# A hybrid decoder layer on one core: the w_out product in seven block products for eight, its transposes and its residual input moved

## The reference

```python
h = rms_norm(x, attn_norm_g)
proj = h @ w_in
...
merged = (jax.nn.sigmoid(g_sb) * (o_sb @ w_branch[:SB_W])
          + jax.nn.sigmoid(g_ds) * (o_ds @ w_branch[SB_W:]))
x = x + merged @ w_out
h = rms_norm(x, ffn_norm_g)
u = causal_depthwise_conv(h @ w_up, conv_w, conv_b)
gate, val = jnp.split(u, 2, axis=-1)
x = x + (jax.nn.silu(gate) * val) @ w_down
```

## Time and profile before

| what | us |
|---|---|
| median of three runs | 1444.48 (1444.48 to 1444.49) |
| the profiled execution | 1446.01 |
| its span | 1444.3 |
| PE busy | 1435.0 (99%) |
| DVE busy | 1097.9 (76%) |
| ACT busy | 827.1 (57%) |
| POOL busy | 437.5 (30%) |

### The profile page before, as it was taken

How to read it: one execution, slowest core, us unless ns; L and a number is a source line. 1 busy time by engine, 2 the same in 40 slices (tenths; PEclk the granted TensorE clock), 3 DMA queues, 4 the chain that set the end, 5 groups by cost and what they waited for, 6 DMA issues and landing times.

```text
span 1444.3 us, 23747 instructions
## 1 busy us (share of the span) xinstructions
PE 1435.0 (99%) x7588; PEld 1228.1 (85%) x7588; DVE 1097.9 (76%) x1468; ACT 827.1 (57%) x1155; POOL 437.5 (30%) x486
## 2 busy tenths in 40 slices
PE   8999999999999999999999999999999999999999
PEld 7888888888888888888888888888888888788887
DVE  6778998886656656765567787777787778899988
ACT  6545677566767766655454554544554545465553
POOL 2310000323232213540015555655556555200000
PEclk9999999999999999999999999999999999999999
DMA  7665665665554555575566666666666665576664
GB/s 246 190 190 162 204 203 179 190 183 176 159 170 149 172 164 183 192 249 184 183 187 177 191 190 190 179 194 189 196 183 187 189 190 188 175 247 205 197 211 146
DMA packets 124358, 272.23 MB, mean 188 GB/s; under 512 B 10784, under 2 KB 10816, under 8 KB 124048
## 3 DMA queue, kind: packets, MB, share of 16 engines
q1 hardware_dynamic: 123520, 269.12, 60.9%
q0 software_dynamic: 464, 2.42, 0.5%
q10 hardware_dynamic: 320, 0.01, 0.0%
HBM read 269.42 MB, written 2.10 MB: 188 GB/s over the span
## 4 chain that ended last, share of the span: by engine, by line
PE 91%; DVE 5%; issue 2%; DMA 1%; POOL 1%; ACT 1%; ACTq 0%; DVEq 0%; SPq 0%; POOLq 0%
PE bank L1950 90%; DVE lo L1149 1%; DVE lo L1549 1%; PE bank L1999 1%; DVE lo L1040 1%; DMA rows_in<-in_attn_norm_g 0%; DMA raw<-in_w_in 0%; POOL u L1914 0%; DMA raw<-in_w_down 0%; ACT hi L583 0%; PE bank L2239 0%; DVE conv L1501 0%; POOL conv L1917 0%; ACT hi L670 0%; DVE y L1639 0%
## 5 line engine op out<-in xcount | busy, mean ns | idle before, releaser
L1040 DVE TENSOR_TENSOR lo<-raw,hi 128x1024 fp32r<-128x1024 f32 (+1 forms) x375 | 484.7, 1298 | 224.1 <-ACT hi L583 223.3
L583 ACT ACTIVATE hi<-raw 128x1024 fp32r<-128x1024 f32 (+1 forms) x375 | 394.0, 1053 | 321.8 <-PE bank L1950 314.7
L1950 PE MATMUL bank<-h2T,hi 128*128 128x512 f32 x1408 | 483.3, 394 | 0.0
L1950 PE MATMUL bank<-h2T,lo 128*128 128x256 f32 x1408 | 376.6, 278 | 0.0
L1950 PEld LDWEIGHTS bank<-h2T,hi 128*128 128x128 f32 x1408 | 257.9, 188 | 53.6
L1950 PE MATMUL bank<-hT,hi 128*128 128x512 f32 (+1 forms) x784 | 273.5, 395 | 0.6 <-DVE qkT L1333 0.6
L1950 PEld LDWEIGHTS bank<-h2T,lo 128*128 128x128 f32 x1408 | 264.4, 188 | 7.8
L1950 PE MATMUL bank<-hT,lo 128*128 128x256 f32 (+1 forms) x784 | 212.9, 281 | 0.0
L1914 POOL TENSOR_TENSOR u<-u,rms_row 128x256 f32<-128x256 f32 x88 | 121.0, 1375 | 239.4 <-DVE u L1491 220.4
L1950 PE MATMUL bank<-hi,ffT 128*128 128x512 f32 x576 | 177.7, 390 | 0.6 <-DVE lo L1549 0.6
L1950 PEld LDWEIGHTS bank<-hT,hi 128*128 128x128 f32 (+1 forms) x784 | 144.0, 187 | 30.5 <-DVE qkT L1333 0.8
(11 more groups left out here) (265 smaller groups left out, 1888.7 us busy)
## 6 DMA issues: line engine op xcount, KB each, us to landing
raw<-in_w_up SPq DMA_DIRECT2D x176, 512.0 KB, 3.8
raw<-in_w_in SPq DMA_DIRECT2D x160, 512.0 KB, 3.6
raw<-in_w_down SPq DMA_DIRECT2D x88, 512.0 KB, 4.4
raw<-in_w_branch SPq DMA_DIRECT2D x32, 512.0 KB, 3.6
raw<-in_w_out SPq DMA_DIRECT2D x32, 512.0 KB, 4.0
raw4h<-in_w_in SPq DMA_DIRECT2D x8, 512.0 KB, 3.6
raw5h<-in_w_in SPq DMA_DIRECT2D x8, 512.0 KB, 4.1
y<-in_x SPq DMA_DIRECT2D x4, 512.0 KB, 6.9
```

The lines of the kernel that those rows point to most:

```text
L583: act.activation(hi[s][:, 0:width], raw[s][:, 0:width], ACT.Copy)\
L1040: dve.tensor_tensor(lo[s][:, 0:width], raw[s][:, 0:width], hi[s][:, 0:width].bitcast(f32), ALU.subtract)\
L1950: return pe.matmul(o, l, r, start=start, stop=stop, skip_group_check=True)
```

## The change

w_out becomes two more blocks, numbered `NB` and `NB + 1`, of eight steps each: four summed pairs (k pairs 0 to 3) alternating with four plain ones (4 to 7). It gets two more `raw` buffers (`raw4m`, `raw5m`), whose first loads wait for the last sigmoids; its sums of `mT` (`left_m`) are made in the branch stage (groups 2 and 3), whose loops are unrolled for that on ACT and DVE. Of x only columns 1024 to 2047 are loaded into `y` at the old place. The first half's banks are copied to `y` by ACT, the far ones added by DVE, and then x's first 1024 columns are added by two accumulating loads from POOL (`x_added`). Of the 16 transposed tiles of `y`, tiles 0 to 3 are made before the last chunk of w_out, the other 12 in pairs behind the first six chunks of the up projection, and the squares for the norm move with them. The first two joins of w_in's last block move from the heads stage to its start. The core of the diff:

```diff
+                        was = (ROW_STEPS + OUT_STEPS)[old // 2]
...
+                        wait_alone(sp, lo_done, (ROWS_AT[2], C_OUT)[stage(step)] - SLOTS + slot + 1)
+                    elif stage(step):
+                        wait_alone(sp, sig_done, 8 * 4)
...
-                    load(slot, raw_rows[slot][:, :],
-                         w_in[kt * P:(kt + 1) * P, ds((2 + NB - 1 - step.m) * BLOCK, BLOCK)])
+                    load(slot, raw_s[stage(step)][slot][:, :],
+                         w[kt * P:(kt + 1) * P, ds(col, BLOCK)])
...
-            with sp.Fori(0, 4) as g:
-                load_group(C_OUT, w_out, CPG * g, GRP * g)
+            for step in OUT_STEPS:
+                load_step(step, w_out, (step.m - NB) * BLOCK)
...
+                if b == NB:
+                    act.activation(y[:, t, h * GRP:(h + 1) * GRP], NEAR[b][o][:, :], ACT.Copy)\
+                        .then_inc(y_out, 1)
+                    return
...
+                    if n >= 2 and j == 3:
+                        left_hi_part(n)
...
+            def square(n, ready, value):
+
+                m, h, t = n // 4, n // 2 % 2, n % 2
+                act.wait_ge(ready, value)
+                act.wait_ge(ss_done, 2 * TH + n - 1)
+                act.activation(junk2[:, t, :], y[:, t, ds(GRP * (2 * m + h), GRP)], ACT.Square,
+                               accum_out=ss[:, t, 2 * m + h:2 * m + h + 1]).then_inc(ss_done, 1)
+
+            for c in range(C_OUT + AHEAD, C_UP + AHEAD):
+                i = c - AHEAD - C_OUT
+                if c == C_UP + 2:
+                    transposed_hi(h2T, KT, 1, [0, 1])
+                chunk_hi(c)
+                if 1 <= i < 5:
+                    merged_hi(3, i - 1)
+                block_out(c)
+                if c == OUT_AT[1] + AHEAD:
+
+                    act.activation(warm[:, :], warm[:, :], ACT.Sqrt).then_inc(passed, 1)
+                if c in (OUT_AT[1] + 19, OUT_AT[1] + 20):
+                    square(c - OUT_AT[1] - 19, x_added[0], 16)
+                if c == C_UP + 2:
+                    transposed_hi(h2T, KT, 1, [2, 3])
...
+                    if not before and 1 <= j < 7:
+                        transposed_hi(h2T, KT, 1, [2 * j + 2, 2 * j + 3])
                     split(C_UP + AHEAD + j, n, 2 * CPG // SLOTS)
                     if before:
                         up_step(n, j)
-                    elif j == 1:
+                    elif j == 0:
+                        square(2, x_added[1], 16)
+                        square(3, x_added[1], 16)
...
+                    if b == NB - 1 and at_ == 2:
+                        join(b, 0)
+                        join(b, 1)
...
-                    if j in (0, 2):
+                    if i and j in (0, 2):
                         join(NB - 1, 2 * i + j // 2)
...
+                    if n >= 2 and j in (0, 1, 2, 4):
+                        {0: sums_whole, 1: sums_diff, 2: sums_rest, 4: sums_lo}[j](n)
+                    weight_sums(c)
...
+            def out_add(m, o, term):
+
+                t, h = o // 2, o % 2
+                cols = y[:, t, (2 * m + h) * GRP:(2 * m + h + 1) * GRP]
+                dve.tensor_tensor(cols, cols, term, ALU.add).then_inc(row_joined, 1)
+
+            def out_sums(m, n):
+
+                one_, five, two, three = far_out[NB + m]
+                if n == 0:
+                    dve.wait_ge(far_copied, 4 * (3 + m) + 4)
+                    dve.tensor_tensor(two[:, :], two[:, :], one_[:, :], ALU.add)\
+                        .then_inc(row_joined, 1)
+                    dve.wait_ge(row_joined, ROW_JOINS + 8 * m + 1)
+                    dve.tensor_tensor(three[:, :], three[:, :], two[:, :], ALU.add)\
+                        .then_inc(row_joined, 1)
...
+            for c in range(C_OUT + AHEAD, C_UP + AHEAD):
+                i = c - AHEAD - C_OUT
+                if c == C_UP + 2:
+                    transposed_lo(h2T, KT, 1, [0, 1])
+                    dve.wait_ge(x_again, 16)
+                    for o in range(4):
+                        wait_full(dve, down_full, 4, 4, o, C_UP)
+                        out_add(1, o, NEAR[NB + 1][o][:, :])
+                    transposed_lo(h2T, KT, 1, [2, 3])
+                chunk_lo(c)
...
+                weight_sums(c)
+                at_ = c - OUT_AT[1]
+                if 0 < at_ < 24 and at_ % 6 == 2:
+                    out_sums(0, at_ // 6)
+                if c == C_UP + 1:
+                    out_sums(1, 0)
...
+                    if not before and 1 <= j < 7:
+                        transposed_lo(h2T, KT, 1, [2 * j + 2, 2 * j + 3])
...
                 mix_body(n, False)
             mix_body(3, True)
+
+            for h in range(2):
+                pool.wait_ge(row_joined, ROW_JOINS + 4 * h + 4)
+                pool.dma_start(y[:, :, h * GRP:(h + 1) * GRP],
+                               x[0, :, h * GRP:(h + 1) * GRP].rearrange("(t p) d -> p t d", p=P),
+                               accum_op=ALU.add).then_inc(x_added[h], 16)
             def column(first, e):
...
                     i.then_inc(w_used, 1)
+                    if last and k == 0 and step.m == NB + 1:
+                        pe.wait_ge(far_copied, S_COPIES)
+                        pe.wait_ge(x_added[0], 16)
+                        transposes(1, range(4), y)
...
+            for step in OUT_STEPS:
+                if step.made is None:
+                    rows_plain(step, step.pair == KT // 2 - 1)
+                else:
+                    rows_summed(step, step.made == S_PAIRS - 1)
             def up_body(n):
                 first_pair = isinstance(n, int)
                 def free_a(ct):
                     if first_pair:
-                        pe.wait_ge(row_done, 6 + max(0, ct - 1))
...
+                            if j < 2:
+                                pe.wait_ge(x_added[1], 16)
+                            else:
+                                pe.wait_ge(row_joined, ROW_JOINS + (16 if j < 4 else 20))
+                            transposes(1, [4 + 2 * j, 5 + 2 * j], y)
+                        if first_pair and b == 0 and j == 6:
```

377 lines of the change are left out of this document (196 added, 181 removed).

## The result

The changed kernel takes 1454.01 us (median; 1453.17 to 1454.33), the kernel before 1444.49 on the same chip: ratio 1.0064, 95% interval [1.0051, 1.0077]. It is 9.5 us slower, where 1.5 us faster was forecast. The profiled span is 1452.6 us, 8.3 more than before; the profiled execution of the kernel before took 1446.01 us, 1.5 above its median, so a difference of the two profiles is not the 9.5 of the medians.

The account below looks back on a forecast made before the run. PE was taken to bound the kernel, busy 99% of the span. -5.45 - 0.5 + 0.3 + 2.4 + 1.4 + 0.4 = -1.45 us off the median 1444.48 gave 1443.0 us, range 1440.4 to 1446.4.

Parts of the forecast that it names:

- The likeliest case: Whole kernel: losses between 3 and 8.8 us against 5.95 saved, counted as no change; chance 0.56, own range 1441.6 to 1446.
- all four cases: Forecast 1443.0 us (0.56), covers hold, middle 1441 (0.33), late accumulating load 1450 (0.06), snowballing opening 1448.6 (0.05).
- The saving: w_out: summed pairs need 7 products for 8, so 24 matmuls fewer at 0.2270 us, 5.45 us gained.
- The joins: Two w_in joins moved to the heads stage's start: VectorE reaches `qkT` earlier, PE's 0.6 us wait shrinks, 0.5 gained.
- The steady state: w_out: its matmuls run at w_in's pace, 0.2283 us against 0.2270; 0.3 us lost, bounds 0 and 0.5.
- Between the halves: Middle of w_out: the table load delays ScalarE's next high part, VectorE and PE; 1.4 us lost, bounds 0.8 and 1.6.
- The opening: Start of w_out: VectorE's prior added work costs nothing; sums waiting for row-block loads delay PE, 2.4 us lost.
- The waits for DMA that I forecast: Start of w_out: VectorE's second-step sums wait for the fifth and sixth row blocks, landing at about 637.
- the opening snowballs: Rival: VectorE enters w_out a chunk late from GpSimd contention, all four loads shared; 8 us for 2.4, 1448.6; chance 0.05.
- The end: w_out into the up projection: VectorE's queue makes `h2T` tiles 4 and 5 late; 0.4 us lost, bounds 0 and 1.2.
- I take 0: End of w_out: x's two accumulating loads of 0.52 MB land in time and cost 0 us.
- The rival on them: Accumulated x lands late for the transposes of tiles 4 to 7 in the up projection; PE loses 7, 1450; chance 0.06.

Follow-up runs that it names:

- b1: The kernel before, with only the two joins of w_in's last block moved to the start of the heads stage: 1444.09 us.
- c5: c3 with the first summed step's sums one chunk sooner: 1443.08 us, against 1445.44 for the kernel before.
- t1: The changed kernel with the early load of the square root's table nine chunks later: 1451.56 us.
- e1: The changed kernel with x's two accumulating loads reduced to one row each: 1450.28 us.
- e5: e3, and w_up's first two loads released two chunks earlier, by the last summed step's buffers: 1447.54 us.
- o7: The changed kernel with the sums of `mT` for the seven products half a group of w_branch earlier: 1450.72 us.
- c2: The changed kernel with the edits of e5, t1 and o7 together: 1443.24 us, against 1444.48 for the kernel before.
- c3: c2 with w_out's first half starting on an eight-product step, its banks A and B exchanged: 1446.61 us, against 1445.34 for the kernel before.
- o5: The changed kernel with the drain of w_branch's banks B put before w_out's third chunk and the s2, s4 sum: 1454.56 us.
- e4: The changed kernel with the last far copy ahead of the late high part of w_up's chunk in ScalarE's queue: 1455.39 us.
- p1: The changed kernel with GpSimd's last two mixing rounds done on only 8 of 256 columns: 1448.89 us.
- o3: The changed kernel with PE's two long waits filled with transposes of the identity into a free bank: 1451.37 us.
- e2: The changed kernel with x's two loads written over `y` instead of added to it: 1454.76 us.
- e3: The changed kernel with x's accumulating loads issued once the direct products lie in `y`, before the partial sums: 1450.09 us.

## Why the prediction was wrong

The likeliest case and the range were missed; the time lies above all four cases.

- **The saving** held: 7588 - 7564 = 24 matmuls. **The joins**, 0.5 us, are not shown: b1's time is 0.4 less with an interval that holds no change, and the wait that they were to remove is back in c5.
- **The steady state**: 1.0 for 0.3, outside its bounds of 0 and 0.5. w_out ran at 0.2297 us a matmul, slower than w_in's 0.2283; a size.
- **Between the halves** held: a wait of 1.17 for 1.4, and it goes with the table load (t1). That t1's time fell by twice as much is in part unexplained.
- **The opening failed**, and the step is the sentence "I cost that at nothing". I set VectorE's added work against its idle time at the durations that it has alone, and then searched the loss further on, in the loads of w_out's rows. The trace of before had both halves of the answer: 13.75 of 20 us busy and 0.96 beside GpSimd for 0.42 alone. The first is 6.25 us idle, and the sum for the last group, 5.2 + 2.7 = 7.9 us, is over it even at the durations alone; 14.3 us at the end of w_branch had 5.2 idle. At the durations beside GpSimd hardly any idle time is left, and what is queued last, the drain, is late by 3.3 us. The waits for DMA that I forecast did not come: the sixth row block landed at 636.74, as forecast near 637, but VectorE got to its sums only at 637.83. The rival "the opening snowballs" had the mechanism in its first half, VectorE late from contention with GpSimd, with a chance of 0.05, and put it at 8 for 2.4; it came to about 6: 3.3, 1.7 of clock, 0.9 of small waits.
- **The end failed**: 6.4 for 0.4. Two steps are wrong. "The wait for the far copies comes out 0.2 us to the good" counted the far copy by PE's progress and not by what is ahead of it on ScalarE, a high part that waits for a load. And of the accumulating loads I asked only when they are needed, and not what they delay: "I take 0" should have been 4.3 (e1). The rival on them looked at PE before `x_added`, where no wait came. The collision is new because x's columns now travel there. Besides, a load of w_up is released a fixed number of chunks ahead, and those of a summed step carry 3, 6, 6 and 6 matmuls for 12, so its lead is shorter; two chunks more of it give 2.0 us (e5). VectorE, which releases these loads, was itself busy for 18.13 and 18.18 of 20 us from 660 to 700, where it was 10.19 and 11.36 before; how much of the short lead is that, no run separates.
- **Not in the sum at all** was the clock: 4.2 us follow the two long waits. The price of a wait was taken as its length.
- **The chances** have a slip: losses "between 3 and 8.8 us" reach up to 1447.3, not 1446. The measured time lies above both.

## What to carry to other kernels

Before added work is costed at nothing, price it at the durations that the same operations have in that company, and follow the last item of that queue to who waits for it. For every transfer that moves, list the other transfers in flight and which queue stands behind them; reordering a queue behind a late load only moves the wait. Fewer matmuls per chunk shorten the lead of every load that is released by chunk count: release the loads sooner in the same edit.

## What the runs showed of the hardware

- After PE's waits of 1.17, 1.52 and 1.55 us (changed kernel, o7, c2) the granted clock stayed at 1.00. After those of 2.94, 3.03, 3.31, 3.90, 4.41 and 4.77 (c3, o5, changed kernel twice, e4, p1) matmuls ran at the lower level for some 3 to 6 us. Transposes of the identity in the wait prevent it (o3).
- VectorE's operations with two inputs in SBUF, where they were slowed beside GpSimd, cost about 0.54 us more whatever their width: 128x256 0.96 for 0.42, 128x512 1.22 for 0.68, 128x1024 1.76 for 1.22 (changed kernel, p1). Not each one that overlaps pays: one of 128x1024 that began at 608.99 in the changed kernel, 0.04 us ahead of GpSimd's, cost 1.21, and GpSimd's operation 1.76 where others of its kind cost 0.74.
- An accumulating load of 0.52 MB from DRAM into SBUF landed in 5.9 and 7.7 us; the second took 29.8% of 12 us of 16 engines, the plain one in its place 17.9% (e2), which landed in 7.5. Two of them issued together landed in 9.1 (e3).
- Beside a load of x in flight, accumulating or plain, the loads of w_up took 7.0 and 7.3 us; without it 4.8 (e1), 5.1 (e3) and 4.9 (e5), and 3.7 in the same stretch of the kernel before.
